# A hybrid decoder trunk on one core: the mLSTM's convolution moved into the attention loop, splits chained from section to section, and a new order at the start

## Chip, core and metric

The kernel runs on one core of one Trainium2 chip. The metric is the device time of one launch in microseconds (us), taken as the median of several runs. Beside it stands one profiled execution, whose trace all rows below come from.

## What is computed

Two layers, each a half-weighted SwiGLU feed-forward, a mixer with three token branches, and a second half-weighted SwiGLU. All in float32; 512 tokens, model width 1024, feed-forward width 2816.

```python
for l in range(DEPTH):
    x = x + 0.5 * swiglu(rms_norm(x, ffn1_norm[l]), ...)
    x = x + hybrid_mixer(rms_norm(x, mix_norm[l]), ...)
    x = x + 0.5 * swiglu(rms_norm(x, ffn2_norm[l]), ...)

# in the mixer, the mLSTM branch:
qk = silu(causal_conv(c_qk, mlstm_conv_w, mlstm_conv_b))   # 512 channels, 4 taps
c_q, c_k = qk[..., :256], qk[..., 256:]
h_c = mlstm_chunked(heads(c_q), heads(c_k), heads(c_v), c_i, log_sigmoid(c_f))
o_c = h_c * sigmoid(c_o)
y = sigmoid(gate_a) * (o_a @ w_branch[0]) + sigmoid(gate_b) * (o_b @ w_branch[1]) + sigmoid(gate_c) * (o_c @ w_branch[2])
```

The other two branches are a gated linear attention (GLA, o_a) and a sparse attention (o_b).

## The kernel before

**Everything is kept transposed**, channels on the 128 partitions and the 512 tokens along a row. Each float32 product is made of three matmuls of float32r, from a high and a low part of either side: weights whi and wlo, data for instance hhi and hlo (lines 1193 to 1195, and 1249 to 1251 for the gated sections). TensorE (PE) does these, one step being three matmuls of 128x128 weights with 512 columns.

**The weights** come through four engines in a chain. SP (line 244) loads a unit of two tiles into one of two buffers `raw`, once POOL's count `lo_done` says that the buffer is free. ACT rounds a tile to its high part (`split_tile` L301, `split_unit` L292), into one of two slots, once PE has done with the tile two before it (`tile_done`). POOL subtracts that from raw (L268) and so gives wlo. PE waits for `lo_done`. In an order written out by hand these splits stand between ACT's other work. DVE takes a unit's product out of its bank and counts it in `unit_free`.

**The sections** of a layer run in this order: gu0, dn0 (first feed-forward), pA, pM0, cq, pM1 (projections of the mixer), cb0, cb1, cb2 (gates and branch products), wo, gu1, dn1. Before gu0, pA and gu1 stands an RMS norm. Its first four tiles run on parts of x that are not yet normed (`pre_split`, L687 and L689, and L663 and L665 for the very first), in two units. In the second tile's middle PE sums the squares over the partitions (L1232, after `sum_part`). ACT makes logarithm and exponential (L340, L342), DVE scales x to fs (L700), ACT and DVE split that again into hhi (L351) and hlo (L713), and the fifth tile on takes these.

**Filled sections.** While the small matmuls of attention, mLSTM and GLA go on, PE does big ones in between. PM1 and CB are plans: after the n-th small piece, so many steps are done; `fill` does them on PE, and on ACT it splits tile T+2 when T has ended. In pM1 they lie within the attention loop over m (16 steps of 4 tiles q; L1411 scores, L1460 transposition of the probabilities, L1441 values); in cb0 in the mLSTM, in cb1 in the GLA. On ACT the first two tiles of cb0, cb1 and cb2 are split after the section before has wholly ended.

**Attention on DVE**: for each m the reciprocal of the sums (L953), the gates (L955), the scaling of four tiles (L960), the maxima of the next m (L937), and the bias of a tile of pM1 (L793) where one has ended.

**Before the mLSTM heads**: PE transposes eight tiles (L1290, into banks 6 and 7 in turn), and the third on waits for ACT's copy (L528) of the one two before. DVE makes the rows of gates, then the convolution: for each of 4 channel tiles one L1013 and three L1016. ACT does the SiLU of each (L531), the sigmoids of c_o (L533), and an exponential of bank 4 (L535). Then PE begins the heads with L1489, which overwrites bank 4, and waits for `em_exp` of L535 and `cv_silu` first. Bank 4 also gives `rt`, a copy by DVE (L1021).

**Before cb1's own part**: DVE finishes the last head (L1056), combines (L803), scans the decays (L1069) and makes the low parts olo (L1064), from ACT's high parts ohi (L561). PE's third fill of cb1 waits for `o_lo`.

**The start.** POOL gives SP the right to both raw buffers at once (L258). ACT issues the loads of the parameters, of x in four pieces and of the constants, then waits for all four pieces (L280) before its first split.

## Time and profile before

| | us |
|---|---|
| median of 3 runs | 2893.99 (2891.21 to 2899.38) |
| profiled execution, its own time | 2890.27 |
| its span (first to last instruction) | 2888.5 |
| PE busy | 2721.1 (94%) |
| DVE busy | 1272.7 (44%) |
| ACT busy | 1020.8 (35%) |
| POOL busy | 1070.3 (37%) |

The mean granted clock of TensorE was 0.987 of full speed. In all rows the times are microseconds from the start of the span, and L12 is line 12 of the kernel. PE is the matmuls, PEld their weight loads, which overlap them. The idle time before an instruction stands in brackets, with what ended it.

### The profile page before, as it was taken

What the parts mean: (1) busy time and instruction counts of PE and PEld (TensorE: products, weight loads), DVE (VectorE), ACT (ScalarE), POOL (GpSimd) and SP (SyncE); (2) the same over time, 40 slices, a digit from 0 to 9 for tenths busy, and PEclk for the clock granted to TensorE, in tenths of its full rate; (3) what the DMA queues carried; (4) which work ended last, traced back from release to release, by engine and by line L of the source; (5) the groups of instructions that cost most, each with busy time, mean ns of one, the idle gap of its engine ahead of it and who ended that gap; (6) DMA issues with size and microseconds to landing.
All of it is one profiled execution on the core that took longest, in us unless ns stands there. A gap on an engine that the chain in (4) does not pass through costs nothing.

```text
span 2888.5 us, 37132 instructions
## 1 busy us (share of the span) xinstructions
PE 2721.1 (94%) x13268; PEld 2165.2 (75%) x13268; DVE 1272.7 (44%) x1596; ACT 1020.8 (35%) x1492; POOL 1070.3 (37%) x450
## 2 busy tenths in 40 slices
PE   6999999999898899999989999999998988999998
PEld 5888877766676787888878888767666767878887
DVE  6333353444546455332353333444454563653322
ACT  3222233554554433222242222344455454332221
POOL 3444444411222344444434444444112223444443
PEclk9999999999999999999999999999999999999999
DMA  3222222210111122223222232232111112222231
GB/s 135 90 99 104 100 88 95 103 45 23 55 55 55 66 99 92 92 97 115 89 74 102 88 108 94 88 109 74 45 34 55 55 55 67 102 92 102 90 118 69
DMA packets 36070, 239.54 MB, mean 83 GB/s; under 512 B 3952, under 2 KB 5232, under 8 KB 13936
## 3 DMA queue, kind: packets, MB, share of 16 engines
q1 hardware_dynamic: 32720, 232.80, 22.9%
q10 hardware_dynamic: 3232, 5.17, 0.5%
q8 instruction: 74, 1.21, 0.2%
q14 instruction: 44, 0.36, 0.0%
HBM read 234.81 MB, written 2.10 MB: 82 GB/s over the span
## 4 chain that ended last, share of the span: by engine, by line
issue 63%; POOL 24%; PE 11%; POOLq 1%; DVE 0%; DVEq 0%
POOL wlo L268 24%; PE bank L1193 4%; PE bank L1195 4%; PE bank L1194 4%; POOLq L267 1%; POOLq L263 1%; DVE hlo L689 0%; DVE x L759 0%; POOL selr L255 0%; DVE hhi L687 0%; POOLq L268 0%; POOLq L259 0%; POOL ones L252 0%; POOL onesm L253 0%; DVEq L759 0%
## 5 line engine op out<-in xcount | busy, mean ns | idle before, releaser
L268 POOL TENSOR_TENSOR wlo<-raw,whi 128x1024 fp32r<-128x1024 f32 (+2 forms) x440 | 1068.7, 2430 | 1799.0 <-ACT whi L301 898.8
L1193 PE MATMUL bank<-hhi,whi 128*128 128x512 f32 x1984 | 796.9, 402 | 52.0 <-POOL wlo L268 38.4
L1195 PE MATMUL bank<-hhi,wlo 128*128 128x512 f32 x1984 | 776.8, 392 | 0.0
L1194 PE MATMUL bank<-hlo,whi 128*128 128x512 f32 x1984 | 775.8, 391 | 0.0
L292 ACT ACTIVATE whi<-raw 128x1024 fp32r<-128x1024 f32 (+1 forms) x232 | 263.7, 1137 | 717.8 <-PE bank L1195 717.8
L1193 PEld LDWEIGHTS bank<-hhi,whi 128*128 128x128 f32 x1984 | 375.6, 189 | 141.3 <-issue 48.5
L1195 PEld LDWEIGHTS bank<-hhi,wlo 128*128 128x128 f32 x1984 | 374.5, 189 | 79.7
L1194 PEld LDWEIGHTS bank<-hlo,whi 128*128 128x128 f32 x1984 | 375.2, 189 | 74.7 <-issue 2.9
L746 DVE TENSOR_TENSOR tmp<-tmp,bank 128x512 f32<-128x512 f32 x80 | 55.0, 688 | 532.6 <-PE bank L1195 532.6
L1193 PE MATMUL bank<-uhi,whi 128*128 128x512 f32 x704 | 274.3, 390 | 0.0
L1194 PE MATMUL bank<-ulo,whi 128*128 128x512 f32 x704 | 273.9, 389 | 0.0
L1195 PE MATMUL bank<-uhi,wlo 128*128 128x512 f32 x704 | 273.9, 389 | 0.0
L301 ACT ACTIVATE whi<-raw 128x1024 fp32r<-128x1024 f32 (+2 forms) x176 | 173.3, 987 | 262.0 <-PE bank L1195 136.4
L736 DVE TENSOR_TENSOR ulo<-tmp,uhi 128x512 f32 (+1 forms) x88 | 212.5, 2415 | 10.1
L389 ACT ACTIVATE tmp<-bank 128x512 f32<-128x512 f32 x80 | 47.9, 599 | 361.3 <-PE bank L1195 346.4
L1249 PE MATMUL bank<-hhi,whi 128*128 128x512 f32 x384 | 159.5, 415 | 16.1 <-POOL wlo L268 16.0
L759 DVE SCALAR_TENSOR_TENSOR x<-bank,x 128x512 f32 x32 | 22.1, 691 | 319.2 <-PE bank L1195 319.2
L689 DVE SCALAR_TENSOR_TENSOR hlo<-x,cur,hhi x48 | 153.5, 3198 | 6.2
L1193 PEld LDWEIGHTS bank<-uhi,whi 128*128 128x128 f32 x704 | 132.1, 188 | 28.8 <-issue 1.2
L1194 PEld LDWEIGHTS bank<-ulo,whi 128*128 128x128 f32 x704 | 132.1, 188 | 27.4
L1195 PEld LDWEIGHTS bank<-uhi,wlo 128*128 128x128 f32 x704 | 132.1, 188 | 27.2
L1250 PE MATMUL bank<-hlo,whi 128*128 128x512 f32 x384 | 151.6, 395 | 0.0
(267 smaller groups left out, 3122.6 us busy)
## 6 DMA issues: line engine op xcount, KB each, us to landing
raw<-gu SPq DMA_DIRECT2D x88, 1024.0 KB, 4.7
raw<-dn SPq DMA_DIRECT2D x32, 1408.0 KB, 5.9
raw<-cb SPq DMA_DIRECT2D x48, 768.0 KB, 4.2
raw<-pM SPq DMA_DIRECT2D x16, 1024.0 KB, 4.7
raw<-cq SPq DMA_DIRECT2D x16, 1024.0 KB, 4.8
raw<-pA SPq DMA_DIRECT2D x12, 1024.0 KB, 4.7
raw<-wo SPq DMA_DIRECT2D x8, 1024.0 KB, 4.7
x<-xT ACTq DMA_DIRECT2D x4, 512.0 KB, 9.7
```

Source lines behind the costliest of these rows:

```text
L268: pool.tensor_tensor(wlo[:, s, 0:w], raw[:, j, lo:lo + w], whi[:, s, 0:w].bitcast(f32), ALU.subtract).then_inc(sem["lo_done"], 1)
L292: A(whi[:, s, 0:w], raw[:, j, lo:lo + w], ACT.Copy).then_inc(sem["hi_done"], 1)
L301: A(whi[:, s, 0:(wa, wb)[s]], raw[:, u % 2, s * wa:s * wa + (wa, wb)[s]], ACT.Copy).then_inc(sem["hi_done"], 1)
L389: A(tmp[:, j], bank[2 * j][:], ACT.Silu).then_inc(sem["silu_ready"], 1)
L689: dve.scalar_tensor_tensor(hlo[:, c], x[:, c], gain, hhi[:, c].bitcast(f32), ALU.mult, ALU.subtract).then_inc(sem["pre_lo"], 1)
L736: dve.tensor_tensor(ulo[:, c], tmp[:, 2 + j], uhi[:, c].bitcast(f32), ALU.subtract).then_inc(sem["ulo_ready"], 1)
L746: dve.tensor_tensor(tmp[:, 2 + j], tmp[:, j], bank[2 * j + 1][:], ALU.mult).then_inc(sem["unit_free"], 1)
L1193: mm(outp, wh, mhi, start=start and k == 0, stop=False)
L1194: mm(outp, wh, mlo, start=False, stop=False)
L1195: i = mm(outp, wl, mhi, start=False, stop=stop and k == len(parts) - 1)
L1249: mm(outp, wh, mhi, start=k == (2 if s else 0), stop=False)
L1250: mm(outp, wh, mlo, start=False, stop=False)
```

## The change

Four edits. (1) The 16 steps of the convolution stand on DVE at the end of the 16 attention steps, one each, and write to `qk`, of which three tiles lie over tiles of the input that are already used up; the SiLUs and the sigmoids of c_o follow ACT's first four transposition copies; bank 4 is copied whole by DVE, the exponential reads that copy, and PE doesn't wait for it. (2) `fill` on ACT goes on with the next section's first two tiles. (3) At the start ACT loads its table first and waits for x only at its squares, and the second raw unit is loaded once x's second piece is there. (4) PE's sum of squares stands behind the 4th, 1st and 2nd step of the second tile for gu0, pA and gu1, instead of the 4th for each. Below, pieces of the same form are left out.

```diff
@@ -136,7 +136,8 @@
-        rt = place("rt", [P, NB, NH])
+        rt2 = place("rt", [P, 2, NB, NH])
+        rt = rt2[:, 0]
@@ -152,7 +153,8 @@
-        row0 = within("row0", last, [NH, S])
+        row0 = zm[0:NH, 3]
+        qk = [within("cvt", last, [P, S])[:], zm[:, 0], zm[:, 1], zm[:, 2]]
@@ -255,7 +257,9 @@
-            pool.sem_inc(sem["lo_done"], credit["lo_done"])
+            pool.sem_inc(sem["lo_done"], 2)
+            pool.wait_ge(x_in[1], 16)
+            pool.sem_inc(sem["lo_done"], credit["lo_done"] - 2)
@@ -271,14 +275,13 @@
             act.wait_ge(sem["const_set"], 6)
+            act.preload_act_table(ACT.Copy)
             act.dma_start(cur[:], t["params"][0]).then_inc(sem["par_ready"], 16)
...
-            for i in range(4):
-                act.wait_ge(x_in[i], 16)
             with act.Fori(0, L) as lay:
@@ -330,6 +333,9 @@
+                            if c % 2 == 0:
+                                act.wait_ge(x_in[c // 2], 16)
+                                act.sem_inc(sem["held"], 1)
                             A(tmp[:, c % 2], x[:, c], ACT.Square).then_inc(sem["sq_ready"], 1)
@@ -402,6 +408,8 @@
                     for T in ended(plan, n):
                         if T + 2 < len(plan[1]):
                             split_tile(name, T + 2)
+                        else:
+                            split_tile({"pM1": "cb0", "cb0": "cb1", "cb1": "cb2"}[name], T + 2 - len(plan[1]))
@@ -509,8 +517,6 @@
                 fill("pM1", PM1, 68)
-                split_tile("cb0", 0)
-                split_tile("cb0", 1)
@@ -526,13 +532,15 @@
                     A(zm[:, 4 + n if n < 4 else 12 + n], bank[6 + n % 2][:], ACT.Copy).then_inc(sem["vm_ready"], 1)
-                    if n >= 4:
-                        act.wait_ge(sem["cv"], me.next("cv", 4))
-                        A(zm[:, n - 4], tmp[:, 3 + n % 2], ACT.Silu).then_inc(sem["cv_silu"], 1)
-                for h in range(NH):
-                    A(zm[:, 8 + h], zm[:, 8 + h], ACT.Sigmoid).then_inc(sem["og_ready"], 1)
+                    if n < 2:
+                        act.wait_ge(sem["cv"], me.at("cv", 16))
+                        for c in (2 * n, 2 * n + 1):
+                            A(qk[c], qk[c], ACT.Silu).then_inc(sem["cv_silu"], 1)
+                    elif n < 4:
+                        for h in (2 * n - 4, 2 * n - 3):
+                            A(zm[:, 8 + h], zm[:, 8 + h], ACT.Sigmoid).then_inc(sem["og_ready"], 1)
                 act.wait_ge(sem["rt_ready"], me.next("rt_ready"))
-                A(st4[:, 0], bank[4][:, NB * NH:2 * NB * NH], ACT.Exp, scale=-1.0).then_inc(sem["em_exp"], 1)
+                A(st4[:, 0], rt2[:, 1].rearrange("p a b -> p (a b)"), ACT.Exp, scale=-1.0).then_inc(sem["em_exp"], 1)
@@ -549,8 +557,6 @@
                 fill("cb0", CB, 24, gate_unit(0))
-                split_tile("cb1", 0)
-                split_tile("cb1", 1)
@@ -597,8 +603,6 @@
                         fill("cb1", CB, 24, gate_unit(1))
-                        split_tile("cb2", 0)
-                        split_tile("cb2", 1)
@@ -965,6 +969,14 @@
                     for q in range(4):
                         fill_group(4 + 4 * m + q)
+                    c, d = m // 4, m % 4
+                    if d == 0:
+                        dve.tensor_scalar(qk[c], zm[:, c], par("convw", 4 * c + 3), par("convb", c), ALU.mult, ALU.add
+                                          ).then_inc(sem["cv"], 1)
+                    else:
+                        dve.scalar_tensor_tensor(qk[c][:, d:S], zm[:, c, 0:S - d], par("convw", 4 * c + 3 - d),
+                                                 qk[c][:, d:S], ALU.mult, ALU.add).then_inc(sem["cv"], 1)
+                    dve.wait_ge(sem["cv"], me.next("cv"))
@@ -1004,21 +1016,10 @@
                 dve.wait_ge(sem["al_out"], me.next("al_out", 2))
-                for n in range(4):
+                for n in range(8):
                     fill_combine(0, n)
-                for c in range(4):
-                    acc = tmp[:, 3 + c % 2]
-                    if c >= 2:
-                        dve.wait_ge(sem["cv_silu"], me.at("cv_silu", c - 1))
-                    dve.tensor_scalar(acc, zm[:, c], par("convw", 4 * c + 3), par("convb", c), ALU.mult, ALU.add).then_inc(sem["cv"], 1)
-                    dve.wait_ge(sem["cv"], me.next("cv"))
-                    for d in (1, 2, 3):
...
-                    fill_combine(0, 4 + c)
                 dve.wait_ge(sem["rt_mm"], me.next("rt_mm"))
-                dve.tensor_copy(rt[:].rearrange("p a b -> p (a b)"), bank[4][:, 0:NB * NH]).then_inc(sem["rt_ready"], 1)
+                dve.tensor_copy(rt2[:].rearrange("p e a b -> p (e a b)"), bank[4][:, 0:2 * NB * NH]).then_inc(sem["rt_ready"], 1)
@@ -1227,7 +1228,7 @@
                         step(2 * u, 1, bank[1][:], hp, k)
-                        if k == KD // 2 - 1:
+                        if k == (3, 0, 1)[f]:
@@ -1480,12 +1481,11 @@
                 pe.wait_ge(sem["rt_ready"], me.at("rt_ready", 1))
-                pe.wait_ge(sem["em_exp"], me.at("em_exp", 1))
                 pe.wait_ge(sem["cv_silu"], me.at("cv_silu", 4))
@@
-                    q, k = zm[r, h // 2], zm[r, 2 + h // 2]
+                    q, k = qk[h // 2][r], qk[2 + h // 2][r]
```

## Rows read from the trace of the kernel before

**Rows 1.** The page: busy times of the engines; the group of ACT's splits (mean ns).

```profile
PE 2721.1 (94%) x13268; PEld 2165.2 (75%) x13268; DVE 1272.7 (44%) x1596; ACT 1020.8 (35%) x1492; POOL 1070.3 (37%) x450
...
L301 ACT ACTIVATE whi<-raw 128x1024 fp32r<-128x1024 f32 (+2 forms) x176 | 173.3, 987 | 262.0 <-PE bank L1195 136.4
```

**Rows 2.** Waits of PE: who waited for whom: total us, times, longest us.

```profile
PE bank L1193 <- POOL wlo L268: 38.4, 15, 20.8
PE bank L1489 <- ACT st L535: 16.7, 2, 8.3
PE bank L1249 <- POOL wlo L268: 16.0, 14, 3.0
...
PE bank L1193 <- DVE hlo L713: 13.3, 12, 1.5
```

**Rows 3.** Timeline, the start: start us, duration us, engine, line, operation, out<-in, count.

```profile
11.31 0.49 DVE L663 TENSOR_SCALAR hhi<-x,cur 128x512 fp32r<-128x512 f32 x1 [11.31 <-DMA x<-xT]
...
15.54 1.28 ACT L301 ACT_TABLE_LOAD   x1 [15.54 <-DMA x<-xT]
...
17.97 5.24 POOL L268 TENSOR_TENSOR wlo<-raw,whi 128x1024 fp32r<-128x1024 f32 x2 [15.89 <-ACT whi L301]
18.42 2.57 DVE L663 TENSOR_SCALAR hhi<-x,cur 128x512 fp32r<-128x512 f32 x1
...
20.84 0.79 PE L1193 MATMUL bank<-hhi,whi 128*128 128x512 f32 x1 [20.84 <-POOL wlo L268]
...
31.87 1.02 PE L1232 MATMUL bank<-tmp,onesm 128*128 128x512 f32 x2
```

**Rows 4.** Windows, the start: stretch, its us, busy of five engines, clock, DMA, GB/s.

```profile
10.00:12.00 2.00, 0.00 (x0) 0.00 (x0) 0.66 (x2) 0.00 (x0) 0.00 (x0) 1.00 1.05 408
```

**Rows 5.** Timeline of ACT, DVE and POOL, norm before pA.

```profile
398.08 0.69 ACT L340 ACTIVATE fs<-bank,eps 128x512 f32<-128x512 f32 x1 [1.22 <-PE bank L1232]
...
411.56 7.07 DVE L713 TENSOR_TENSOR hlo<-fs,hhi 128x512 fp32r<-128x512 f32 x8
...
413.38 2.89 POOL L268 TENSOR_TENSOR wlo<-raw,whi 128x1024 fp32r<-128x1024 f32 x1 [3.49 <-ACT whi L301]
```

**Rows 6.** Timeline of ACT and PE, before the mLSTM heads.

```profile
743.00 0.63 ACT L531 ACTIVATE zm<-tmp 128x512 f32<-128x512 f32 x1 [2.51 <-DVE tmp L1016]
...
760.10 1.28 ACT L535 ACT_TABLE_LOAD   x1
...
761.82 0.79 PE L1489 MATMUL bank<-rows,selr 64*128 64x512 f32 x1 [8.35 <-ACT st L535]
```

**Rows 7.** Windows around L1489, columns as in rows 4: PE, PEld, DVE, ACT, POOL.

```profile
757.00:762.00 5.00, 0.18 (x1) 0.19 (x2) 0.00 (x0) 4.96 (x8) 0.00 (x0) 0.51 0.00 0
762.00:767.00 5.00, 5.00 (x10) 2.85 (x11) 0.51 (x1) 2.66 (x8) 1.80 (x1) 0.50 0.00 0
```

**Rows 8.** Timeline of DVE: a softmax step, and two convolutions.

```profile
598.88 0.18 DVE L953 RECIPROCAL st<-st 128x4 f32<-128x4 f32 x1 [0.51 <-ACT tmp L495]
...
740.65 2.32 DVE L1016 SCALAR_TENSOR_TENSOR tmp<-zm,cur,tmp 128x511 f32<-128x511 f32 x3
...
748.06 3.92 DVE L1016 SCALAR_TENSOR_TENSOR tmp<-zm,cur,tmp 128x511 f32<-128x511 f32 x3
```

**Rows 9.** Timeline of DVE and PE, and a window, where cb1 begins.

```profile
727.80 1.21 DVE L983 TENSOR_TENSOR_SCAN tmp<-ones,tmp 4x512 f32<-4x512 f32 x1
...
837.68 2.23 DVE L1069 TENSOR_TENSOR_SCAN bcum<-ones,tmp 128x512 f32<-128x512 f32 x1 [0.16 <-DVE y L803]
...
842.64 2.50 DVE L1064 TENSOR_TENSOR olo<-zm,ohi 128x512 fp32r<-128x512 f32 x4
...
839.00:842.50 3.50, 3.50 (x9) 2.72 (x10) 3.50 (x2) 0.75 (x2) 2.53 (x1) 0.51 0.00 0
...
844.78 0.39 PE L1249 MATMUL bank<-hhi,whi 128*128 128x512 f32 x1
...
846.14 0.39 PE L1249 MATMUL bank<-ohi,whi 128*128 128x512 f32 x1
```

3 lines of the change are left out of this document (removed).

## The prediction

> **What bounds the kernel now.** The page's busy times come first: TensorE is busy for 2721.1 of 2888.5 us [rows 1]. So the time is the matmuls' own, plus the stretches in which they wait, plus what they lose at the lower clock. The second view is PE's list of waits [rows 2]; only what it names can be won by reordering. The largest entry that a reordering can take away is L1489, the first matmul of the mLSTM heads. It waited twice (once in a layer) for ACT's exponential of L535, 16.7 us in all, 8.3 at the longest. Next are the waits of L1193 and L1249 for POOL's low parts (38.4, of which 20.8 is the start, and 16.0) and that for DVE's low parts hlo (13.3). Third, the timeline around each place tells who is late behind the one named. The layers run the same stages, so a place of layer 0 is counted twice, and the start once.
>
> **1. The wait at L1489.** The reader should follow ACT's column [rows 6]. Its transposition copies are cheap, but it stands behind DVE's convolution for each SiLU (743.00, 2.51 us idle), and swaps its function table back and forth between SiLU and the gates' sigmoid. The four sigmoids of the output gate come last, and behind them a load of 1.28 at 760.10 for the exponential that frees bank 4. PE reaches L1489 at 753.5, and begins it at 761.82, after 8.35 [rows 6]. Moreover the granted clock is 0.51 in 757 to 762 and 0.50 in 762 to 767 [rows 7], that is 1.2 instead of 2.4 GHz, after these 8 us of waiting. After the change the convolution is done before the loop of transpositions begins. ACT then has one load for four SiLUs, one for four sigmoids, which the gates share, and one for the exponential. That exponential reads SBUF, and PE no longer waits for it. What PE still needs (rt_ready, cv_silu, vm_ready) is ready before it arrives: rt is copied by DVE right after the transposition, and the last SiLU comes about six copies earlier. Sum: 8.35 for the stall, plus 5 of the 5.0 us in 762:767 run at half clock, which is 2.5, makes 10.9. The wait of L1249 for POOL in the middle of this loop comes from ACT's split standing behind a SiLU that waits for DVE; it is worth 1.1 (16.0 over 14 waits, rows 2). Against it, the second and third copy now have a table load of 1.28 and two functions ahead of them, so I charge 0.5 for copies and splits that come late. I take **11.5 per layer**, from 7 (a stall of 3 us remains, with part of its low clock) to 12.
>
> **2. The convolution's 16 steps inside the attention loop.** Each is one DVE instruction; three of them took 2.32 us at 740.65, 0.77 each, and 3.92 at 748.06 [rows 8], so one of those was held for 1.6. The tightest place of the attention for DVE is 598.88, with 0.51 us of idle before the next softmax step [rows 8]. A free step exceeds that by 0.3, and behind it DVE waits again for PE's scores, so nothing reaches PE. A held one may. Waiting on its own semaphore blocks the next maxima and reciprocals in DVE's queue, behind which stand the scaled probabilities that PE transposes. Bounds for the 16 are 0 to 5 per layer (three or so that are held by 1.6). I take 0.4, as nearly all have over 1 us of idle.
>
> **3. Chained splits.** cb0's first split goes into the 15th attention step, before the fourth copy: 0.1 of PE, at most the 0.99 of a split [rows 1]. There is nothing to win, as PE's first use comes after the transpositions. cb2's splits move too, but PE reaches cb2 only after the GLA outputs, so the gain is 0. cb1 is where a stall goes: PE stood for POOL up to 3.0 us [rows 2], here just before 839, and then 839 to 842.5 ran at clock 0.51 [rows 9]. With the split earlier, PE starts 3.0 us earlier and warm, and gets to the first matmul with ohi (846.14 before) after 24 matmuls of 0.227 (six in 1.36 us, rows 9), at 841.4. **What is late next is olo.** DVE does the combination, two scans from 837.68 to 842.6, then four subtractions, done at 845.14 [rows 9]. They don't begin earlier (the gate's sigmoid even gets later by a split, some 0.9). They gain only what POOL held the scans: the first took 2.23, where a free scan of 512 takes 1.21 [rows 9], so the two gain up to 2.5, and POOL's next subtraction (1.80 in 762:767, rows 7) may take 1.8 of it back. So olo is ready at 843.2 to 845.0. PE's first matmul with ohi comes then instead of at 846.14: 1.1 to 2.9 us are won, not 4.8. The new stall (2 to 3.6 us) is as long as the one before which the clock fell; a fall would cost 1.7. I take **1.0**, from -0.8 to 4.8.
>
> **4. The sum of squares earlier in pA and gu1.** The ones-matmul goes from behind the 4th step of the second tile to behind the 1st (pA) and the 2nd (gu1), 2.0 and 1.4 us earlier. ACT can use 1.2 of it: so long did it stand idle, its table loaded, before the logarithm at 398.08 [rows 5]. At its end DVE writes hlo from 411.56, POOL's subtraction at 413.38 (released by a tile of PE, which doesn't move) cuts in, and PE waits for the fifth part. One or two more parts get done ahead of POOL, each three matmuls of 0.227 = 0.7. I take 0.7 at each of the two norms, **1.4 per layer**, from 0 to 2.4.
>
> **5. The start.** ACT's first split waited for all of x (15.54), then a table load; POOL began at 17.97, PE at 20.84 [rows 3]. Now the load is at the very front, ACT waits for raw alone, and raw's second unit is held back until x's second piece has landed. At 408 GB/s [rows 4] its 1024 KB free 2.6 us for x: the first piece is there at 8.7 instead of 11.31, the second (1.4 later) at 10.1. POOL, whose queue stands behind that piece too, starts then, and PE at about 12.8: 8 us earlier. But DVE has to write sixteen parts of x and add eight squares before PE's L1232 (31.87). Its L663 beside POOL's subtraction lasted 2.57 [rows 3]; these two blockages stay. The 16 parts and the sum, and with them L1232, thus move only with x, by 2.6. PE arrives early and waits at L1232. I take **2.5**, from 0.5 to 8. The table load ahead of ACT's DMA issues (1.28) hides behind raw's first unit, which keeps the DMA busy; uncovered it costs 1.3. The later raw unit is covered by some 10 us of PE's first tiles. SP has nothing behind it.
>
> **Sum.** Per layer 11.5 - 0.4 - 0.1 + 1.0 + 1.4 = 13.4; twice 26.8; with the start 29.3. The profiled execution took 2890.27 us for a span of 2888.5, and would take 2861.0. The median of the runs lies 3.7 above it, at 2893.99, and would be 2864.7. I say **2865**.
>
> **A rule weighed.** The rows show DVE instructions on SBUF held beside POOL's subtraction (L663 for 2.57, rows 3; a convolution step for 1.6 more, rows 8). The Trainium skill (SBUF — State Buffer, section Who interferes with whom) says that a DVE instruction with two SBUF inputs, or in a two-port mode, and a GpSimd instruction reading SBUF exclude each other, whoever is first holding the other for its whole length. Twelve of the sixteen steps read two SBUF tensors, so by that rule the move into the attention can also delay the low parts there, which speaks against this change; for DVE's side the trace agrees with 2.57 us. By the rule the sum would go towards rival C, by the rows it stays at 0.4.
>
> **Rivals.**
> A. *The stalls go in full.* olo is in time, the clock stays up, and the start gives its 8 us: 4.8 - 1.0 twice and 5.5 more are 13, giving 2852. For it: POOL's two blockages are most of the scans' length. Against it: the chains of points 3 and 5. Chance 0.15.
> B. *ACT becomes the bound of the transposition loop.* With its loads and functions ahead of the copies, PE waits at the vm copies or for late splits, 4 us a layer: 2873. For it: between two copies PE has 12 matmuls of 0.227 and four transpositions, some 3.2 us, and the second copy has a load (1.28) and two SiLUs of 0.63 [rows 6] ahead, 2.5. Against it: the loads of table get fewer, from one at each change between SiLU and sigmoid to three. Chance 0.17.
> C. *Slower: POOL holds the convolution steps in the attention.* If each of the 32 is held for 1.6 and lasts 0.77, with 0.5 of slack, PE loses 1.9 each, 60 us: 2925. It decides from 38 us on, 1.2 for each step. For it: rows 8 and 3. Against it: POOL's subtractions there come after ten splits only, and DVE waits for PE behind each. The rule weighed above is the mechanism of this rival. Chance 0.03.
> D. *It doesn't do what it says.* The wait at L1489 only changes its name, to rt_ready or the SiLUs, at its old length: the rest gives 29.3 - 2 x 10.9 = 7.5, so 2886. Chance 0.05, as nothing that feeds them is late in the rows.
> My forecast has 0.60.
>
> **How the numbers follow.** The bounds of the parts reach from a gain of 12 to one of 47, but not together. Forecast, A and B take 2852 to 2873; widened by a few us for the unknowns and the median's own scatter of 8 us among the runs, the range is 2850 to 2877. A measurement of this kernel tells 0.3% (8.7 us) from no change. Faster: forecast, A and B, 0.92; within: D, 0.05; slower: C, 0.03.
>
> **What would show it.** In the profile after: L1489 no longer among the waits, no half clock near 757, three table loads between the attention and the first head; L1249 waiting for olo of L1064 instead of wlo, once a layer, 2 to 3.6 us; PE's first matmul near 13, but a wait of about 3 us at L1232 until about 29.3; gaps at L1193 for hlo shorter by some 0.7. It is wrong if L1460 or L1411 wait more in the attention, or if the vm copies of L528 grow in PE's list.

## The result

The kernel before took 2894.97 us (median; 2891.21 to 2899.38), the changed one **2847.22 us** (2843.56 to 2850.83). The ratio is 0.984, with a 95% interval of 0.9824 to 0.9855. The change makes the kernel 1.6% faster, 48 us. I had forecast 2865 with a range of 2850 to 2877: the sign was right, the gain 18 us too small, and the measured time lies 3 us below the range. It also lies below rival A (2852).

The profiled execution of the changed kernel took 2845.81 us for a span of 2844.0 (before: 2890.27 and 2888.5), and its mean granted clock was 0.990 (0.987). TensorE's busy time fell from 2721.1 us [rows 1] to 2714.7 (first table of the page of the changed kernel), though it runs the same 13268 matmuls. So 6 of the 44.5 us of the spans are matmuls that run at full clock now, and most of the rest are waits. (The medians differ by 3 us more than the two profiled spans; all that follows is read from the spans.)

```profile
PE 2714.7 (95%) x13268; PEld 2162.2 (76%) x13268; DVE 1259.6 (44%) x1596; ACT 1013.8 (36%) x1487; POOL 1073.8 (38%) x450
```

The waits of TensorE, as in rows 2, are now these (who waited for whom: total us, times, longest us):

```profile
PE bank L1194 <- POOL wlo L272: 28.7, 15, 13.5
...
PE bank L1250 <- DVE olo L1065: 11.3, 4, 3.3
...
PE bank L1250 <- POOL wlo L272: 7.0, 9, 1.0
PE bank L1233 <- DVE tmp L686: 6.2, 2, 3.3
...
PE bank L1291 <- ACT zm L534: 3.2, 2, 1.6
...
PE bank L1194 <- DVE hlo L717: 0.9, 2, 0.5
```

Lines have moved: L1193, L1249, L1489, L1064, L713 and L268 of before are L1194, L1250, L1489, L1065, L717 and L272 of after. The 16.7 us of L1489 are gone and have no successor of their size. POOL's waits at the big matmuls fell by 9.7 and at the gated ones by 9.0, and the waits for hlo, which DVE writes at the norms, fell from 13.3 to 0.9. New are olo (11.3, of which 6.6 is the wait before cb1, twice 3.3; the rest was there before) and the ones-matmul L1233 at the start (2.8).

**Where the time went, stage by stage.** The list of waits doesn't hold what the clock costs. So I paired each matmul of a kernel with the same one of the kernel before, and read how much earlier it starts. The number is the gain within a stage in us, minus is a loss; "1 / 2" is layer 0 / layer 1. Differences outside the named stages, under 0.7 each, are left out. Some experiments of the next section stand in the same table, under their numbers there.

```
stage                       after        3 norm order  4 no chain    7 mLSTM       10 olo first  8 em only
start, to 70 us             1.41         -1.26          2.67          -1.23        2.37          0.36
norm before pA              2.10 / 2.75  2.73 / 2.71    2.11 / 2.75   0.05 / 0.02  2.72 / 2.71   0.01 / 0.03
attention's first 30 us     2.15 / 0.81  0.02 / -0.04   1.30 / 0.80   1.10 / 0.18  2.16 / 0.13   1.27 / 2.05
rest of the attention       0.03 / 0.01  0.04 / 0.05   -0.01 / 0.01   0.01 / 0.07  -0.01 / 0.04 -0.03 / -0.02
mLSTM's transpositions     12.85 / 12.76 -0.05 / -0.09 12.81 / 12.72 12.80 / 12.72 12.80 / 12.76 4.35 / 4.35
start of cb1               -0.28 / 1.32  0.02 / 0.03   -1.22 / 0.00  -0.02 / 0.01  4.85 / 4.86   0.15 / -2.46
GLA, cb2 (two stages)      -0.16 / -1.25 0.01 / -0.03  -1.12 / -3.81 -3.90 / -3.63 -2.14 / -3.82 0.08 / 0.21
norm before gu1             3.58 / 5.17  3.31 / 3.31    2.18 / 2.30   1.87 / 1.88  3.60 / 3.58  -0.01 / -0.01
norm of layer 1's first gu0 1.01         1.13           2.17          2.18         0.20         -0.45
all                        44.5         11.4           35.2          23.8         46.7           9.6
```

The large blocks are the transpositions (25.6 of 44.5) and the four norms of pA and gu1 (13.6). The start of experiments 3 and 7 has no edit and still stands 1.2 behind the kernel before, with a stretch of low clock at 63.0 that that one hasn't; so a microsecond or two in a stage can be the clock's alone.

**mLSTM's transpositions.** ScalarE and TensorE of the changed kernel, in the timeline (start us, duration, engine, line, operation, count, [idle before <- releaser]), to read beside rows 6:

```profile
722.92 1.28 ACT L538 ACT_TABLE_LOAD   x1
...
728.12 1.28 ACT L541 ACT_TABLE_LOAD   x1
...
739.97 0.67 ACT L423 ACTIVATE tmp<-bank,cur 128x512 f32<-128x512 f32 x1
740.53 1.08 ACT L534 ACTIVATE zm<-bank 128x512 f32<-128x512 f32 x2
741.63 1.28 ACT L543 ACT_TABLE_LOAD   x1
743.21 0.21 ACT L543 ACTIVATE st<-rt 128x16 f32<-128x16 f32 x1 [0.30 <-DVE rt L1022]
```

```profile
745.83 0.49 PE L1489 MATMUL bank<-rows,selr 64*128 64x512 f32 x1
```

Three table loads, as forecast, and the exponential done 2.4 us before TensorE gets there. The granted clock, which was 0.51 and 0.50 around L1489 [rows 7], stays up (windows of the changed kernel; columns as in rows 4, then clock, DMA share, GB/s):

```profile
743.00:748.00 5.00, 5.00 (x19) 3.31 (x20) 0.18 (x1) 2.50 (x6) 1.82 (x1) 1.00 0.45 157
748.00:753.00 5.00, 5.00 (x23) 3.94 (x21) 0.69 (x1) 3.34 (x7) 1.54 (x1) 1.00 0.01 2
```

**The norm before pA.** This is where the forecast was too small. The apply pass (`fs`, eight instructions of DVE) and POOL's subtractions of the kernel before:

```profile
400.75 9.68 DVE L700 SCALAR_TENSOR_TENSOR fs<-x,cur,tmp 128x512 f32<-128x512 f32 x8 [6.83 <-ACT tmp L342]
```

```profile
401.99 2.43 POOL L268 TENSOR_TENSOR wlo<-raw,whi 128x1024 fp32r<-128x1024 f32 x1 [3.96 <-ACT whi L301]
407.42 2.46 POOL L268 TENSOR_TENSOR wlo<-raw,whi 128x1024 fp32r<-128x1024 f32 x1 [3.01 <-ACT whi L301]
```

and the same of the changed kernel, to read beside rows 5:

```profile
395.46 0.69 ACT L346 ACTIVATE fs<-bank,eps 128x512 f32<-128x512 f32 x1
```

```profile
398.13 7.53 DVE L704 SCALAR_TENSOR_TENSOR fs<-x,cur,tmp 128x512 f32<-128x512 f32 x8 [5.62 <-ACT tmp L348]
405.58 1.28 DVE L711 TENSOR_TENSOR z<-bank,tmp 128x512 f32<-128x512 f32 x2
406.78 8.60 DVE L717 TENSOR_TENSOR hlo<-fs,hhi 128x512 fp32r<-128x512 f32 x8
```

```profile
400.58 2.55 POOL L272 TENSOR_TENSOR wlo<-raw,whi 128x1024 fp32r<-128x1024 f32 x1 [3.95 <-ACT whi L304]
406.01 2.41 POOL L272 TENSOR_TENSOR wlo<-raw,whi 128x1024 fp32r<-128x1024 f32 x1 [2.89 <-ACT whi L304]
411.97 2.87 POOL L272 TENSOR_TENSOR wlo<-raw,whi 128x1024 fp32r<-128x1024 f32 x1 [3.55 <-ACT whi L304]
```

Everything of TensorE and POOL is 1.41 us earlier at this place (407.42 became 406.01). DVE's pass begins 2.62 earlier, so 1.2 more, which is the idle time of the logarithm in rows 5, as forecast. But it ends 4.8 earlier, because it now takes 7.53 instead of 9.68. In the kernel before the last two instructions, from 406.88 on, took 3.55 us together. One of 0.7 was done, and the eighth came up at 407.55, when POOL had just begun at 407.42; it stood until POOL's end at 409.88. Now the eighth is through before 406.01. So a head start of 1.2 turned into 3.4 us, relative to TensorE. TensorE had less to win than that: its list of waits for this stretch holds 2.2 us for hlo in the kernel before, and 0.4 in the changed one. The same count holds at all four norms of pA and gu1: in the kernel before two of the eight instructions take 2.9 us and the pass 9.68, in the changed kernel one does and the pass takes 7.53.

**The start.** To read beside rows 3, DVE, ScalarE, POOL and TensorE of the changed kernel:

```profile
6.83 1.28 ACT L304 ACT_TABLE_LOAD   x1 [3.44 <-DMA raw<-gu]
```

```profile
8.73 0.49 DVE L667 TENSOR_SCALAR hhi<-x,cur 128x512 fp32r<-128x512 f32 x1 [8.73 <-DMA x<-xT]
...
11.10 2.56 DVE L667 TENSOR_SCALAR hhi<-x,cur 128x512 fp32r<-128x512 f32 x1
13.70 2.74 DVE L669 SCALAR_TENSOR_TENSOR hlo<-x,cur,hhi 128x512 fp32r<-128x512 f32 x1
```

```profile
10.57 5.32 POOL L272 TENSOR_TENSOR wlo<-raw,whi 128x1024 fp32r<-128x1024 f32 x2 [8.48 <-ACT whi L304]
```

```profile
13.52 0.79 PE L1194 MATMUL bank<-hhi,whi 128*128 128x512 f32 x1 [13.52 <-POOL wlo L272]
...
28.92 2.08 PE L1233 MATMUL bank<-tmp,onesm 128*128 128x512 f32 x2 [2.82 <-DVE tmp L686]
```

x's first piece is there at 8.73 (forecast 8.7), TensorE begins at 13.52 (12.8), and waits 2.82 at the ones-matmul, which comes at 28.92 (29.3). That is 2.95 us earlier than in rows 3. Not all of this is the change's: three other kernels with the old start (experiments 3, 7 and 8) have this matmul at 31.26 to 31.30, and seven more profiles with the new one at 28.96 to 29.27. Between the two starts lie 2.0 to 2.95 us.

### The profile page after: what moved, and what is told of

Its sections match the earlier page's. It is cut to its first block, busy times and chain, and to the rows that moved or that the text cites. A ratio compares the mean times of both kernels' runs of the same rounds, so it can differ in the third digit from the quotient of the medians.

```text
span 2844.0 us, 37156 instructions
## 1 busy us (share of the span) xinstructions
PE 2714.7 (95%) x13268; PEld 2162.2 (76%) x13268; DVE 1259.6 (44%) x1596; ACT 1013.8 (36%) x1487; POOL 1073.8 (38%) x450
## 3 DMA queue, kind: packets, MB, share of 16 engines
q10 hardware_dynamic: 3232, 5.17, 0.5%
## 4 chain that ended last, share of the span: by engine, by line
issue 62%; POOL 25%; PE 11%; POOLq 1%; DMA 0%; DVE 0%; ACTq 0%; ACT 0%; DVEq 0%
POOL wlo L272 25%; PE bank L1194 4%; PE bank L1196 4%; PE bank L1195 4%; POOLq L271 1%; POOLq L267 1%; DMA x<-xT 0%; DVE hlo L693 0%; DVE x L763 0%; DVE hhi L691 0%; POOLq L272 0%; POOL vcm L256 0%; POOL selr L257 0%; ACTq L281 0%; ACT L278 0%
## 5 line engine op out<-in xcount | busy, mean ns | idle before, releaser
L272 POOL TENSOR_TENSOR wlo<-raw,whi 128x1024 fp32r<-128x1024 f32 (+2 forms) x440 | 1072.3, 2438 | 1751.0 <-ACT whi L304 863.5
L1194 PE MATMUL bank<-hhi,whi 128*128 128x512 f32 x1984 | 797.2, 402 | 30.4 <-POOL wlo L272 28.7
L1196 PE MATMUL bank<-hhi,wlo 128*128 128x512 f32 x1984 | 777.3, 392 | 0.0
L1195 PE MATMUL bank<-hlo,whi 128*128 128x512 f32 x1984 | 776.3, 391 | 0.0
L1194 PEld LDWEIGHTS bank<-hhi,whi 128*128 128x128 f32 x1984 | 376.0, 190 | 118.7 <-issue 36.5
L1194 PE MATMUL bank<-uhi,whi 128*128 128x512 f32 x704 | 274.4, 390 | 0.0
L1250 PE MATMUL bank<-hhi,whi 128*128 128x512 f32 x384 | 158.5, 413 | 7.1 <-POOL wlo L272 7.0
L1194 PEld LDWEIGHTS bank<-uhi,whi 128*128 128x128 f32 x704 | 132.1, 188 | 28.7 <-issue 1.2
L1252 PE MATMUL bank<-hhi,wlo 128*128 128x512 f32 x384 | 150.6, 392 | 0.0
```

The lines of the kernel that those rows point to most:

```text
L272: pool.tensor_tensor(wlo[:, s, 0:w], raw[:, j, lo:lo + w], whi[:, s, 0:w].bitcast(f32), ALU.subtract).then_inc(sem["lo_done"], 1)
L1194: mm(outp, wh, mhi, start=start and k == 0, stop=False)
L1195: mm(outp, wh, mlo, start=False, stop=False)
L1196: i = mm(outp, wl, mhi, start=False, stop=stop and k == len(parts) - 1)
L1250: mm(outp, wh, mhi, start=k == (2 if s else 0), stop=False)
L1252: i = mm(outp, wl, mhi, start=False, stop=bool(s) and k in (1, 5))
```

## The experiments

Each kernel was timed against the kernel before on the same chip, except the last, of which there is a single profiled execution. "After" in the headings is the changed kernel. Parts are numbered as the points of the prediction: 3 is the chained splits, 4 the sums of squares, 5 the start.

**1. The sums of squares put back (after, without part 4).**

```diff
-                        if k == (3, 0, 1)[f]:
+                        if k == (3, 3, 3)[f]:
```

> The changed kernel with the sum of squares back behind the 4th step in all three norms. Asked: how much of the gain of 44.5 us (span) is due to the earlier sums. Between neighbouring places of the two traces PE gained 2.7 and 3.1 us in the two pA norms and 4.1 and 5.6 in the two gu1 norms, 15.5 in all, where the prediction had 2.8. If these are the norms' own doing, this kernel is slower than the changed one by 13 to 16 us (span about 2858 to 2860), and the gaps at L1194 for hlo come back (1.2 and 1.8 us a norm). If the prediction's size was right and the rest came from shifts of the clock's low stretches, it is slower by 3 only (span about 2847).

Measured: 2856.24 us (2852.7 to 2860.97), ratio 0.9874 [0.9855, 0.9893]: 9.0 more than the changed kernel, where I had expected 13 to 16. In the stages before pA the gain was 0.02 and 0.01 (2.10 and 2.75 in after), so it goes in full there. Before gu1 1.88 and 1.89 stayed. They are the clock's: the kernel before has a stretch of low clock at 1122.4 and one at 2552.5, of 3.4 us each, and this kernel has none there. The kernel of experiment 7 hasn't either, and shows the same 1.87 and 1.88 without part 4. Of the 13.6 us of the four stages part 4 thus has 9.8 in the changed kernel, and the clock 3.8. DVE's pass in this kernel took what it took before:

```profile
396.29 9.68 DVE L704 SCALAR_TENSOR_TENSOR fs<-x,cur,tmp 128x512 f32<-128x512 f32 x8 [6.83 <-ACT tmp L348]
```

**2. The sums placed between (after, with part 4 done by less).** This tells whether the gain grows with the distance or comes at a threshold.

```diff
-                        if k == (3, 0, 1)[f]:
+                        if k == (3, 2, 2)[f]:
```

> The changed kernel with the sum of squares behind the 3rd step (3, 2, 2): 0.7 us earlier than before, instead of 2.0 and 1.4. Lock theory: what counts is that the eighth scaling of fs begins before POOL's subtraction of tile 4 (before it began 0.13 us after that, at 407.55 against 407.42, and lasted 2.89); 0.7 is enough for that, so nearly the whole gain stays: within 3 us of the changed kernel (span 2844 to 2847), 11 or more below the kernel with late sums. Linear theory (each 0.7 us earlier gives 0.7): half of what separates the changed kernel from the one with late sums is lost, 7 us if that is 15.

Measured: 2850.91 us (2848.1 to 2852.81), ratio 0.9852 [0.9836, 0.9869]. The stages before pA gave 2.69 and 2.63, those before gu1 3.53 and 5.15 (2.10, 2.75, 3.58 and 5.17 in the changed kernel): all of the gain, though the ones-matmul is only one step, 0.7 us, earlier than in the kernel before. The pass has the short length here too:

```profile
397.67 7.53 DVE L704 SCALAR_TENSOR_TENSOR fs<-x,cur,tmp 128x512 f32<-128x512 f32 x8 [6.15 <-ACT tmp L348]
```

Relative to POOL's second subtraction it begins 7.35 us ahead (405.02 less 397.67). In experiment 1 it is 6.68 (402.97 less 396.29), in the kernel before 6.67, in the changed one 7.88. So 0.7 of head start is enough, and a gain in proportion would have been half of the changed kernel's. The total is 3.7 above the changed kernel all the same. It lost that in stages without an edit, where this kernel has stretches of low clock that the changed one hasn't (468.0, 580.6, 840.1).

**3. The norm order alone (before, with part 4 only).**

```diff
-                        if k == KD // 2 - 1:
+                        if k == (3, 0, 1)[f]:
```

> The kernel before with nothing but the earlier sums (3, 0, 1). If the norms are independent of the rest: faster than before by 11 to 16 us (span 2873 to 2877). The prediction's size: by 3 (span 2885.7). If the gain needs the other edits (the phase of the clock), it lies between.

Measured: 2881.16 us (2878.9 to 2884.05), ratio 0.9958 [0.9942, 0.9975], 12.8 us under the median of the kernel before on the same chip. The four stages gave 2.73, 3.31, 2.71 and 3.31, which makes 12.1. So part 4 is worth 12 us and not the 2.8 of my sum. This kernel has its stretches of low clock at the gu1 norms as the kernel before (1117.7 and 2541.1), so none of the 3.31 is the clock's. The waits for hlo before pA and before gu1, 2.2 us at each norm in the kernel before, are gone; at gu1 0.6 of a wait for POOL goes with them (2.8 became 2.2).

**4. Without the chain (after, the splits of cb0, cb1 and cb2 back at their old places).**

```diff
-                        else:
-                            split_tile({"pM1": "cb0", "cb0": "cb1", "cb1": "cb2"}[name], T + 2 - len(plan[1]))
...
+                split_tile("cb1", 0)
+                split_tile("cb1", 1)
```

> The changed kernel with the first splits of cb0, cb1 and cb2 back behind the end of the section before. The prediction: where cb1 begins the wait for POOL (3.0 us, then a low clock) comes back and the wait for olo (3.3 us) goes; the two differ by 1.0 us a layer, so this kernel is 2 us slower than the changed one, and its attention 0.1 faster. The changed kernel's own trace gives -0.3 and +1.3 us for the two layers there, so 1 us. A rival, that chaining is worth its 3.0 us and the clock, gives 8 to 10 us slower.

Measured: 2857.11 us (2855.12 to 2859.71), ratio 0.988 [0.9863, 0.9896]. At the start of cb1 this kernel stands 0.9 and 1.3 behind the changed one, about the 1.0 per layer of the forecast. The wait of before is back there (in the window of 812 to 840 us):

```profile
PE bank L1254 <- POOL wlo L272: 3.0, 1, 3.0
```

But the whole is 9.9 worse, not 2. The stages that the edit doesn't touch lost the rest: against the changed kernel 3.5 in GLA and cb2, and 4.3 at the two gu1 norms. This kernel has 18 stretches of low clock with 79.5 us in all, the changed one 14 with 59.1. I come back to that below.

**5. The start alone (before, with part 5 only).**

```diff
-            pool.sem_inc(sem["lo_done"], credit["lo_done"])
+            pool.sem_inc(sem["lo_done"], 2)
+            pool.wait_ge(x_in[1], 16)
+            pool.sem_inc(sem["lo_done"], credit["lo_done"] - 2)
...
+            act.preload_act_table(ACT.Copy)
...
-            for i in range(4):
-                act.wait_ge(x_in[i], 16)
...
+                            if c % 2 == 0:
+                                act.wait_ge(x_in[c // 2], 16)
+                                act.sem_inc(sem["held"], 1)
```

> The kernel before with the new start alone. The prediction: 2.5 us faster (DVE's chain moves only with x). The changed kernel's trace: L1233 (the sum of squares) 2.95 us earlier, of which 1.7 went to the low clock at 28.8, and after the first norm 1.4 to 4.4 us are left, depending on whether the clock falls there and at 59. So 1.5 to 4.5 us. A rival, that PE's 7.3 us at its first matmul are won, gives 7 to 8.

Measured: 2892.47 us (2887.92 to 2896.7), ratio 0.9998 [0.9987, 1.0008]. The interval holds no change, where I had expected 1.5 to 4.5. At 70 us it was 2.79 ahead, as forecast, at the mLSTM stage 4.80, and then it lost 0.68, 1.59 and 2.47 at the heads and in the GLA stages, where it has no edit. It ended level. 17 stretches of low clock make 92.0 us there, against 13 with 74.9 in the kernel before.

**6. raw not held back (after, without POOL's wait for x's second piece).**

```diff
-            pool.sem_inc(sem["lo_done"], 2)
-            pool.wait_ge(x_in[1], 16)
-            pool.sem_inc(sem["lo_done"], credit["lo_done"] - 2)
+            pool.sem_inc(sem["lo_done"], credit["lo_done"])
```

> The changed kernel, but POOL gives both of raw's load credits at once, so that raw's second unit no longer waits for x's second piece. By the prediction's theory (the 1024 KB of that unit at about 408 GB/s take 2.6 us away from x, and the end of the start hangs on x through DVE's sixteen parts) DVE's first part starts at about 11.3 instead of 8.7 and the ones-matmul at about 31.7 instead of 28.9: the gain at the start falls from 2.9 to about 0.3, and the kernel takes 2 to 3 us more than the changed one, 2850. The rival is that the gain at the start comes from ACT's shorter queue (load first, no wait for all of x); then the ones-matmul stays within 0.5 us of 28.9. Beyond the first 70 us I expect no stage to differ except where the clock's low stretches fall elsewhere, 1.7 us each.

Measured: 2858.32 us (2854.7 to 2859.09), ratio 0.9877 [0.986, 0.9893]. The timelines of DVE and TensorE:

```profile
11.24 1.85 DVE L665 TENSOR_SCALAR hhi<-x,cur 128x512 fp32r<-128x512 f32 x1 [11.24 <-DMA x<-xT]
```

```profile
30.69 1.12 PE L1231 MATMUL bank<-tmp,onesm 128*128 128x512 f32 x2 [2.81 <-DVE tmp L684]
```

The first part of x is at its old time (11.24; 11.31 before), so it is raw's second unit that held x up. The ones-matmul is 1.8 later than in the changed kernel, less than the 2.8 that I expected. Held against all kernels with either start (31.26 to 31.87 with the old one, 28.92 to 29.27 with the new), its 30.69 leaves 1.4 to 1.8 for the held unit and 0.6 to 1.2 for the shorter queue of ScalarE and POOL. At 70 us this kernel is even with the changed one (1.30 and 1.41), since that one had a stretch of low clock at 59.5. So the 11 us by which the whole is worse aren't there at 70 us; they arose later. It has 21 stretches of low clock, 81.6 us.

**7. The mLSTM parts alone (after, without parts 3, 4 and 5).**

```diff
-                        if k == (3, 0, 1)[f]:
+                        if k == KD // 2 - 1:
...
(the chain and the start undone, as in 4 and 5)
```

> The kernel before with the convolution in the attention, the new places of SiLUs and sigmoids and the exponential from SBUF, without chained splits, new start and earlier sums. Prediction: 11.5 us a layer less 0.5 for the attention, 22. By the changed kernel's trace the stretch from the end of the attention to the first head gives 12.8 us in each layer, so 25.6 without any loss in the attention (span 2863). If the 16 steps cost something in the attention that the clock's shifts hid, it is less than 23.

Measured: 2866.54 us (2865.39 to 2869.02), ratio 0.9911 [0.9894, 0.9928]. The transpositions gave 12.80 and 12.72, the same as in the changed kernel, and the attention behind its first 30 us 0.01 and 0.07. The sixteen steps of the convolution cost the attention nothing that shows.

**8. em from SBUF alone (before, the exponential reading SBUF, and TensorE not waiting for it; the copy of the whole of bank 4 is left out below).**

```diff
-                A(st4[:, 0], bank[4][:, NB * NH:2 * NB * NH], ACT.Exp, scale=-1.0).then_inc(sem["em_exp"], 1)
+                A(st4[:, 0], rt2[:, 1].rearrange("p a b -> p (a b)"), ACT.Exp, scale=-1.0).then_inc(sem["em_exp"], 1)
...
-                pe.wait_ge(sem["em_exp"], me.at("em_exp", 1))
```

> The kernel before with one thing only: bank 4 is copied whole and PE doesn't wait for the exponential of L535. The convolution, SiLUs and sigmoids stay. PE then waits for the fourth SiLU (ended 756.6 before) instead of 761.6: the stall of 8.35 becomes 3.2, 5 us a layer less, and the low clock is the same or one stretch shorter: 10 to 15 us in all. If ACT's sigmoids matter for something else before the first head (the decay exponentials of L543 come behind them), the gain is less, since ACT reaches L543 no earlier: then the stall only moves behind L1489 to the wait for d_exp and 3 to 5 us in all are won.

Measured: 2888.35 us (2880.73 to 2892.09), ratio 0.998 [0.9971, 0.999], less than the 10 to 15 us that I expected. The transpositions gave 4.35 twice. The mechanism of rival D is what one sees here, though not at the old length. With the wait for the exponential gone, one of 3.15 us for the last SiLU takes its place, and the clock is low behind it as before (TensorE and the windows of this kernel):

```profile
755.12 0.79 PE L1489 MATMUL bank<-rows,selr 64*128 64x512 f32 x1 [3.15 <-ACT zm L532]
```

```profile
755.00:760.00 5.00, 4.88 (x9) 2.81 (x10) 0.00 (x0) 4.94 (x8) 0.00 (x0) 0.50 0.00 0
```

**9. em back in the bank (after, the exponential reading bank 4 and TensorE waiting for it).** This is the other half of experiment 8.

```diff
-                A(st4[:, 0], rt2[:, 1].rearrange("p a b -> p (a b)"), ACT.Exp, scale=-1.0).then_inc(sem["em_exp"], 1)
+                A(st4[:, 0], bank[4][:, NB * NH:2 * NB * NH], ACT.Exp, scale=-1.0).then_inc(sem["em_exp"], 1)
...
+                pe.wait_ge(sem["em_exp"], me.at("em_exp", 1))
```

> The changed kernel with the exponential of em reading bank 4 again and PE waiting for it before the first matmul of the first head, as in the kernel before; the convolution stays in the attention loop. In the trace of the changed kernel that exponential starts at 743.21 and PE comes to the head at 745.83, so if the gain of 12.8 us per layer comes from ACT's queue being short by then, the wait is over before PE asks, and the mLSTM stage keeps 12 to 13 us of gain; total 2847 within the clock's scatter of 4. The rival: the gain comes from PE no longer waiting for ACT at all; then the wait shows up again with 2 to 8 us per layer, and the total is 2851 to 2863.

Measured: 2852.46 us (2848.71 to 2855.4), ratio 0.9855 [0.9839, 0.9872]. The transpositions gave 12.84 and 12.78, as much as without the wait. TensorE comes to the first head at 744.75, and what it waits for was over at 742.29:

```profile
742.11 0.18 ACT L543 ACTIVATE st<-bank 128x16 f32<-128x16 f32 x1 [0.31 <-DVE rt L1022]
...
744.75 0.49 PE L1490 MATMUL bank<-rows,selr 64*128 64x512 f32 x1
```

So the wait that the diff takes away is worth nothing once ScalarE's queue is short. The 12.8 are the work of moving the convolution and regrouping the functions; no run separates these two. Taking the wait away is worth 4.35 only where they haven't been moved. The total was 5.2 above the changed kernel, in stages with no edit (17 stretches of low clock, 75.8 us).

**10. olo first (after, the four subtractions ahead of the scans).** The forecast's point 3 names olo as the next in line at cb1. This puts it first.

```diff
+                out_low(1, 8)
...
-                out_low(1, 8)
```

(the first line stands ahead of the two scans of L1070, the second was behind them)

> The changed kernel with DVE's four subtractions of olo ahead of the two scans of the decays, where cb1 begins. In the changed kernel PE stood 3.3 us at L1250 for olo of L1065 once in each layer, with a low clock right after (827.5 to 831.0), as the prediction said. Theory: olo is then done about 2.5 us earlier, before POOL's subtraction of 822.4 gets in, and PE arrives at 822.8 and doesn't wait: 3.3 for the stall and 1.7 for the clock, 5 us a layer, 10 in all (span about 2834). Rival: the scans, later by 2.7, make the first distances of the GLA late, and the stall only moves to L1543 (2.1 us now): 3 us or nothing.

Measured: **2842.48 us** (2840.68 to 2843.58), ratio 0.9819 [0.9803, 0.9835]. This is the fastest kernel of the study, by 4.7 us of median, though its interval and that of the changed kernel (0.9824 to 0.9855) overlap a little. The start of cb1 gained 4.85 and 4.86, against -0.28 and 1.32. The changed kernel at cb1, where DVE has to write olo while POOL subtracts (DVE, POOL, TensorE):

```profile
819.39 1.41 DVE L1070 TENSOR_TENSOR_SCAN bcum<-ones,tmp 128x512 f32<-128x512 f32 x1 [0.15 <-DVE y L807]
820.72 1.19 DVE L1070 TENSOR_TENSOR_SCAN bcum<-ones,vcm 128x512 f32<-128x512 f32 x1
821.95 4.11 DVE L1065 TENSOR_TENSOR olo<-zm,ohi 128x512 fp32r<-128x512 f32 x4
```

```profile
822.43 1.86 POOL L272 TENSOR_TENSOR wlo<-raw,whi 128x768 fp32r<-128x768 f32 x1 [2.72 <-ACT whi L304]
```

```profile
826.11 0.50 PE L1250 MATMUL bank<-ohi,whi 128*128 128x512 f32 x1 [3.28 <-DVE olo L1065]
...
827.63 0.63 PE L1250 MATMUL bank<-ohi,whi 128*128 128x512 f32 x1
```

A matmul takes 0.63 from 827.63 on instead of 0.39: the clock has fallen. Its window, and the same one of the kernel with olo first (TensorE only; then clock, DMA share, GB/s):

```profile
828.00:832.00 4.00, 4.00 (x13) 0.63 0.00 0
```

```profile
818.21 2.70 DVE L1065 TENSOR_TENSOR olo<-zm,ohi 128x512 fp32r<-128x512 f32 x4 [0.15 <-ACT ohi L567]
...
820.94 1.22 DVE L1071 TENSOR_TENSOR_SCAN bcum<-ones,tmp 128x512 f32<-128x512 f32 x1
```

```profile
820.00:824.00 4.00, 4.00 (x20) 1.00 0.48 183
824.00:828.00 4.00, 4.00 (x19) 1.00 0.00 0
```

With olo done at 820.9 there is no wait and the clock stays up. Of the 8.7 us that this gained over the changed kernel at cb1, 4.6 were given back in the GLA and cb2 stages (-3.82 instead of -1.25, -2.14 instead of -0.16), where the same pauses now had low clock behind them. The rival of my expectation, that the stall only moves to L1543, doesn't hold: the waits there are 11.8 us in all, 11.7 in the changed kernel.

**11. The changed kernel once more.** A second profile, to see how much of the clock is chance.

> The changed kernel itself, profiled once more. If the stretches of low granted clock are set by the kernel's own pauses, they begin at the same places as in its first profile (568.1, 827.5, 878.7, 899.2 in the first layer), within a few tenths of a us. If they fall by chance, some are missing and others are new, and the differences of 1.7 us per stretch between kernels outside the changed stages mean nothing. I expect most (two thirds) at the same places and some at others.

Measured: 2846.18 us, span 2844.3 (2844.0 in the first profile). Of the first profile's 14 stretches of low clock 12 are there again, 0.3 to 0.4 us later, one stands at 1978.2 instead of 1988.0, and one is missing. It is that from 1438.5 to 1445.3, which begins in the wait of L1233 before layer 1's first projection; the wait was 3.3 us long in the one profile and 3.2 in the other. TensorE's window after it, first profile, then second:

```profile
1440.00:1445.00 5.00, 5.00 (x10) 0.50 0.00 0
```

```profile
1440.00:1445.00 5.00, 4.68 (x19) 1.00 0.00 0
```

So the places are mostly the kernel's own, and the same pause can go either way. Stage by stage this profile differs from the first in two places: 0.05 instead of 1.01 at layer 1's first gu0, and 2.07 instead of 0.81 at the attention's entry of layer 1, which is where the two stretches are that differ.

The first difference has a sign that one wouldn't expect. At layer 1's first gu0 the profile with the low stretch is the one that gained, and DVE's pass says why, first profile, then second:

```profile
1444.65 7.53 DVE L704 SCALAR_TENSOR_TENSOR fs<-x,cur,tmp 128x512 f32<-128x512 f32 x8 [4.83 <-ACT tmp L348]
```

```profile
1444.27 9.68 DVE L704 SCALAR_TENSOR_TENSOR fs<-x,cur,tmp 128x512 f32<-128x512 f32 x8 [4.00 <-ACT tmp L348]
```

With TensorE at half clock POOL's subtraction comes at 1447.54 instead of 1445.37, while the pass begins only 0.4 later, and it meets one subtraction instead of two. The order of this norm isn't changed by any edit. In the thirteen profiles the nine with a low stretch there have the pass of 7.53 and the four without one that of 9.68. At the attention's entry it is the place that counts: the stretch at 1978.2 lies ahead of TensorE's wait of 1.8 us for DVE (L1428), which then shrinks to 0.2, the one at 1988.0 lies behind it, and the wait stays.

## Why the forecast fell short, point by point

**Point 1, the wait at L1489: right, and 1.4 per layer too small.** The stall, its cause (ScalarE's queue of SiLU, sigmoid and loads) and the half clock behind it are as forecast, and experiments 8 and 9 show the cause from both sides. 12.8 was measured for 11.5 less 0.1 for cb0. By the paired matmuls 8.4 of it come at L1489 and 2.6 behind it, from the clock, where I took 8.35 and 2.5. What I had too small lies ahead of L1489, 1.8 for my 0.6 (1.1 less 0.5): the matmul of POOL's wait begins 1.4 earlier, one of the transpositions 0.4. The copies and splits that I charged 0.5 for came late by nothing that reached TensorE: in the changed kernel its waits between 715 and 775 us are 1.6 for a vm copy and 0.9 for an olo, in the kernel before 1.8 and 0.9. This rules out rival B. Experiment 9 corrects one thing in my reading. I put "PE no longer waits for it" first, and it is worth nothing. Rival D is false for the change, and true for the one line alone, at 3.15 us instead of the old 8.35.

**Point 2, the convolution in the attention: 0 instead of -0.4 per layer.** Three of the 32 steps were held: one of L974, 2.59 us at 583.61 beside a subtraction of POOL from 583.52 to 585.91, and two of L977, 2.72 at 692.73 and 2.71 at 2102.20. The others took 0.53 to 0.75. TensorE's waits for the scaled probabilities (L1460, now L1461), which I had named as a sign of being wrong, grew from 6.5 to 7.3 us, and yet the rest of the attention lost nothing (0.03 and 0.01). Rival C is ruled out by this and by experiment 7. The rule that I weighed there agrees with these three steps, but such meetings were rarer than rival C needs, and the slack behind DVE covered them.

**Point 3, the chain: right in its place, and half of the forecast's size.** olo is next, and the wait is 3.28 (2 to 3.6 forecast). The gain over the kernel without the chain is 0.9 and 1.3, but the forecast's 1.0 per layer was meant against the kernel before, and there it was -0.28 and 1.32: the clock fell behind the wait in layer 0 (827.5), which I had priced at 1.7, while in layer 1 it fell only further on, at 2247.5, and was paid in the next stage (GLA and cb2, -1.25). Rival A, olo in time, is false for the change. It is true for the order of experiment 10, with 4.85, and this is the upper bound of 4.8 that point 3 had.

**Point 4, the norms: the step that failed.** I wrote "One or two more parts get done ahead of POOL, each three matmuls", 0.7 per norm and at most 2.4 a layer. The four stages gave 2.7, 3.3, 2.7 and 3.3 alone (experiment 3), and 13.6 in all in the changed kernel, some of it the clock's (experiment 1). My upper bound was below what the list of waits held: TensorE waited 2.2 us for hlo at each of these norms, 4.4 a layer. The head start of 1.2 was right. I carried it to the end of hlo as 1.2, and didn't follow POOL through the pass in between. There, the eighth instruction of fs came up 0.13 us behind the start of POOL's subtraction of 407.42, and a DVE instruction that reads two SBUF tensors stands for the whole 2.5 of POOL's. A head start of 1.2, and by experiment 2 also one of about half of that, gets it through. The gain isn't an amount of time but one instruction less that is held: all profiles with the earlier sums have one held at each of these norms, all with the late ones two. The Trainium skill ("SBUF — State Buffer", section "Who interferes with whom") gives the rule by which it can be read: outside its two-port modes a DVE instruction with at most one input in SBUF doesn't contend with GpSimd, and one with two inputs in SBUF contends with a GpSimd instruction that reads SBUF. The trace agrees: in the changed kernel L711, which reads a bank and `tmp`, took 0.68 at 406.18 beside POOL's 406.01 to 408.42, and an instruction of fs, whose inputs are all in SBUF, took 2.88 at 400.79 beside POOL's 400.58 to 403.13. I had cited this rule in the forecast for the convolution, where it cost nothing, and not used it here, where it decided.

**Point 5, the start: 2.0 to 2.95 at the ones-matmul for 2.5.** All times of the chain came within 0.8 us. Only the load at the very front brought nothing: there is a load at 2.10, and another at 6.83 all the same. At 60 us the kernel stood 2.98 ahead; the stage's 1.41 at 70 us is this less a stretch of low clock at 59.5.

**The sum.** It was 29.3 against 44.5 measured. The norms make 10.8 of the difference (13.6 for 2.8), the transpositions 2.8 (25.6 for 22.8). The attention makes 3.8 (3.0 for my -0.8). cb1 takes 1.0 off, the start 1.1, all else 0.4. These are 14.9 of 15.2. With the norms at the 12.1 of experiment 3 the forecast would have been 2855.4, inside my range; what brings the time down to 2847 is the rest. The 3.0 at the attention's entry and the 1.0 at layer 1's first gu0 come from no edit in these stages. In layer 0 a low stretch of 6.8 us at 583.1 became one of 3.4 at 568.1, ahead of TensorE's wait of 1.8 for DVE's pc, and the wait went with it. That these 4.0 came as a gain is no merit of the change, as far as any run shows. Experiments 5 to 8 move the same stages by up to 2.2 us, and GLA and cb2 by up to 4.1, without an edit in them.

**The clock as a term of its own.** The parts do add up where the edits are, stage by stage. Over the kernel they don't: one part alone or one undone differed in the total by up to 11 us from what its own stages gave (experiments 4, 6 and 9 lose 5 to 11 us against the changed kernel for edits that cost 0 to 2.3 in their own stages). In the kernels seen, the stretches of low clock are 3.4 to 10.2 us long, cost at most half of that where TensorE is busy, and number 12 to 21, with 45 to 92 us in all. The changed kernel has 59.1 us of them, the kernel before 74.9. The stretch at L1489 (10.2 in each layer) is a part of that, and it is what the change took away by its own doing. For the rest, a low stretch isn't a cost alone: where it shifts POOL against DVE, as at layer 1's first gu0, the stage can gain by it (experiment 11). And no run here shows what makes a pause of 2.5 to 3.5 us cost a low stretch in one kernel and not in another. I leave that open. A forecast of this kernel should therefore have been wider for the clock alone, by an estimated 5 us to either side (from the 5 to 11 us of experiments 4, 6 and 9). Mine wasn't, and that and the norms are why it missed.

## What to carry to other kernels

Where a pass of one engine is held by another that works in bursts, its cost is counted in bursts that it meets: lay the pass and the bursts side by side at the new start time and count again, since a tenth of a microsecond can decide over two. Of two edits at one wait, try which of them the wait hangs on before crediting the one that names it. Expect small reorderings to move stretches of low clock elsewhere, some microseconds each way, and judge an edit by its own stage as well as by the whole.

## What the runs showed of the hardware

- The granted clock was low in 12 to 21 stretches of 3.4 to 10.2 us per kernel. Two profiles of the same kernel shared 12 of 14, and after a pause of 3.2 to 3.3 us the clock fell in one of them and stayed up in the other.
- Loads share the bandwidth so plainly that one can be bought with another: the 1024 KB of raw's second unit, taken off the queue, brought x's first piece from 11.24 to 8.73 us.
- The scaling fs took 0.74 to 0.75 us free and 2.88 to 2.90 where it came up just behind the start of POOL's subtraction, and the pass of eight took 9.7 with two held and 7.5 with one, in all thirteen profiles.
- A low stretch of TensorE's clock can shorten a stage: at layer 1's first gu0 it delayed POOL's subtraction by 2.2 us, and DVE's pass met one instead of two.
- A scan over two SBUF tensors is held by POOL like an elementwise instruction: 2.81 instead of 1.2 us at 822.08 in the kernel with olo first, beside a subtraction at 821.22 to 823.80.
- The preload of a table for Copy at 2.10 us didn't save the load of 1.28 before the first copy at 6.83 in the changed kernel.
